# A hybrid decoder step: 120 unused words behind the constants, taken from the end of the big SBUF buffer

## The reference

```python
def expert(acc, ew):
    w1, b1, w2, b2, g_col = ew            # w1: 1024 x 2048, w2: 1024 x 1024, float32
    hh = xt @ w1 + b1
    glu = jnp.minimum(hh[:, 0::2], SWIGLU_LIMIT)
    lin = jnp.clip(hh[:, 1::2], -SWIGLU_LIMIT, SWIGLU_LIMIT)
    y = ((lin + 1.0) * (glu * jax.nn.sigmoid(SWIGLU_ALPHA * glu))) @ w2 + b2
    return acc + g_col[:, None].astype(y.dtype) * y, None
```

## Time and profile before

| | |
|---|---|
| median of three runs | 1518.68 us (1517.12, 1518.68 and 1520.63) |
| the profiled execution | 1514.24 us, of it 1512.4 us in the span of the profile |
| PE busy | 1357.4 us (90% of the span) |
| DVE busy | 472.7 us (31%) |
| ACT busy | 175.8 us (12%) |
| DMA over the span | 490.56 MB in 96,722 packets, 324 GB/s on the mean |

### The profile page before, as it was taken

One profiled execution on the slowest core, in us unless ns is written; L12 is line 12 of the kernel. 1 busy time (PEld: TensorE's weight loads), 2 busy tenths in 40 slices (PEclk: granted clock), 3 DMA queues, 4 the chain that ended last, 5 costly groups with the idle time before them and its releaser, 6 DMA issues.

```text
span 1512.4 us, 20016 instructions
## 1 busy us (share of the span) xinstructions
PE 1357.4 (90%) x8119; PEld 649.6 (43%) x8119; DVE 472.7 (31%) x1080; ACT 175.8 (12%) x343; POOL 49.5 (3%) x47
## 2 busy tenths in 40 slices
PE   8999769879997989999999988989989889899896
PEld 6667534334486444333333333333333333333332
DVE  1856556733124252122122113112221131122213
ACT  1143101221012430000000000000000000000002
POOL 0000210000000420000000000000000000000000
PEclk9999889889999999999999999999999999999999
DMA  9111545546366669999999999999999999999996
GB/s 360 38 62 48 196 153 196 203 140 251 145 244 220 237 264 416 397 413 415 417 418 414 420 415 415 420 415 417 418 414 419 416 415 420 415 417 418 415 419 238
DMA packets 96722, 490.56 MB, mean 324 GB/s; under 512 B 9307, under 2 KB 14527, under 8 KB 61754
## 3 DMA queue, kind: packets, MB, share of 16 engines
q1 hardware_dynamic: 94074, 468.80, 77.2%
q0 software_dynamic: 2304, 20.97, 3.6%
q10 hardware_dynamic: 296, 0.11, 0.0%
HBM read 483.91 MB, written 6.04 MB: 324 GB/s over the span
## 4 chain that ended last, share of the span: by engine, by line
PE 40%; DMA 18%; DVE 6%; SPq 3%; issue 2%; ACT 1%; POOL 1%; DVEq 0%
PE ps L2025 17%; DMA arena<-in_w_e 17%; PE ps L2062 13%; PE ps L2018 2%; SPq L1457 2%; PE ps L2050 1%; PE ps L2074 1%; DVE arena L2590 1%; DVE arena L2600 1%; DVE arena L2597 1%; DVE arena L2598 1%; DMA arena<-in_cache_mem_k 1%; PE ps L2090 1%; PE ps L2104 1%; SPq L1453 1%
## 5 line engine op out<-in xcount | busy, mean ns | idle before, releaser
L2025 PE MATMUL ps<-arena 128*64 128x512 f32 x2048 | 455.9, 595 | 29.1 <-DMA arena<-in_w_e 28.5
L2025 PEld LDWEIGHTS ps<-arena 128*64 128x64 f32 x2048 | 149.3, 137 | 311.7 <-issue 284.3
L2062 PE MATMUL ps<-arena 128*64 128x512 f32 x952 | 216.5, 609 | 1.2 <-ACT arena L2277 1.2
L2062 PEld LDWEIGHTS ps<-arena 128*64 128x64 f32 x952 | 78.0, 142 | 138.3 <-issue 125.4
L2597 DVE TENSOR_SCALAR arena<-ps 128x1024 f32<-128x1024 f32 x15 | 18.4, 1225 | 252.7 <-PE ps L2025 252.7
L2018 PE MATMUL ps<-arena 96*128 96x512 bf16 x96 | 39.6, 540 | 46.1 <-DVE arena L2590 46.1
L2609 DVE COPY arena<-ps 128x512 f32<-128x512 f32 x15 | 10.4, 692 | 218.8 <-PE ps L2062 218.8
L2615 DVE TENSOR_TENSOR res<-res,ps 128x512 f32<-128x512 f32 x60 | 41.3, 688 | 116.4 <-PE ps L2074 116.4
L1071 PE MATMUL ps<-arena 32*4 32x512 f32 x640 | 47.1, 641 | 14.9 <-PEq L1149 10.5
L2011 PE MATMUL ps<-arena 128*128 128x128 bf16 x768 | 54.2, 222 | 2.0 <-DVE arena L2564 2.0
L2011 PEld LDWEIGHTS ps<-arena 128*128 128x128 bf16 x768 | 49.7, 99 | 14.3 <-issue 12.2
(11 more groups left out here) (554 smaller groups left out, 1361.4 us busy)
## 6 DMA issues: line engine op xcount, KB each, us to landing
arena<-in_w_e SPq DMA_DIRECT2D x383, 1024.0 KB, 18.7
arena<-in_w_in SPq DMA_DIRECT2D x8, 1380.0 KB, 17.6
arena<-in_cache_mem_k SPq DMA_DIRECT2D x8, 1024.0 KB, 8.9
arena<-in_w_out SPq DMA_DIRECT2D x2, 2048.0 KB, 8.8
arena<-in_w_xk SPq DMA_DIRECT2D x1, 4096.0 KB, 16.0
arena<-in_w_xv SPq DMA_DIRECT2D x1, 4096.0 KB, 13.5
arena<-in_w_xq SPq DMA_DIRECT2D x1, 4096.0 KB, 23.3
arena<-in_cache_mem_v SPq DMA_DIRECT2D x1, 4096.0 KB, 16.5
```

What stands on the lines that cost most here:

```text
L2025: last = pe.matmul(ps[64 * x:64 * x + 64, c, :], xe[:, k, 64 * x:64 * x + 64], weights[x][:, c * 512:(c + 1) * 512], start=False, stop=(k ...
L2062: last = pe.matmul(ps[64 * x:64 * x + 64, 4 + c, :], aT[:, k, 64 * x:64 * x + 64], weights[x][:, j * D + c * 512:j * D + (c + 1) * 512], s ...
```

## The change

The table of constants gets 120 words more in each partition (480 bytes), which nothing reads, and `arena` gets 120 words less at its end. No instruction is added, taken away or moved, and no place inside `arena` changes, except one that is counted from its end (`AT_MORE = ARENA - ...`, a place for 1024 words of cached rotary keys), whose address stays as it was.

```diff
 C_HEAD = C_SUB + 1
-C_ALL = C_HEAD + H
-
-ARENA = 45680 + 3072 + 188
+C_ALL = C_HEAD + H + 120
+
+ARENA = 45680 + 3072 + 188 - 120
```

## The result

The changed kernel takes 1497.62 us (median of four runs, 1495.04 to 1505.40) against 1517.95 us (1517.12 to 1520.63): a ratio of 0.9872 with a 95% interval from 0.9833 to 0.9910. The forecast was 1518.7 us with a range down to 1513.5; the gain is 16 to 20 us. The profiled execution took 1497.29 us, of it 1495.5 us in the span, 16.9 us less than before.

The account below looks back on a forecast made before the run. The prediction took the expert stage to be bound by its weight queue at 417 GB/s. Its terms summed to 0 us on the profiled 1514.24 us; placed on the runs' median, the forecast was 1518.7 us, range 1513.5 to 1522.0.

Parts of the forecast that it names:

- the other parts: Longer constants load, moved stored states and PE, DVE and ACT operands moved by 480 bytes: each was to cost nothing.
- the cover of 86 us: Stored states land at 183.7 us, first read at 270.1 us; even a load 9.4 us longer was to cost nothing.
- From this I take the gain for a packet in the ring as nothing: Expert loop's weight landings: aligned ring places gain 0 us, bounded by 13.2 us of gain and 6.6 us of loss.
- block 7: The w_in block landing on a multiple of 512: 418.6 ns a packet, no cheaper than block 3's 416.9 ns.
- The sign of failure that I had named: Prediction fails if whole packets of 4096 and 8192 bytes profit from a clean start and a clean end together.
- The whole excess goes: Rival, expert loop: all 3.4 ns a packet come from landing, 13.2 us faster, 1505.5 us; chance 0.05 including a larger case.
- my line of prices: Packet price fitted from small and w_in packets: 8.2 ns fixed plus 0.03702 ns a byte, 236.5 ns for loop packets.
- One beat less: Rival, ring packets: an aligned start saves 32 bytes, 1.18 ns each, 4.6 us in all, 1514.1 us; chance 0.09.

Follow-up runs that it names:

- e9: Changed kernel plus six groups of 16 loads behind its last store; w_in blocks took 418.8, 415.8, 418.8 and 426.5 ns from 0, 128, 224 and 240.
- e7: Changed kernel plus ten groups of 20 loads behind its last store, varying start and length; 8192-byte packets took 309.0 ns from 0 and 314.6 from 32.
- e5: Kernel before with 24 unused words, so arena starts 128 past a multiple of 512; 1514.86 us against 1515.76, ratio 0.9991.
- e6: Kernel before with 56 unused words, so arena starts 256 past a multiple of 512; 1499.70 us against 1515.76, ratio 0.9879.
- e1: Kernel before with 8 unused words, so arena starts 64 past a multiple of 512; 1514.38 us against 1516.57, ratio 0.9991.

## Why the prediction was wrong

**What held.** The expert stage is bound by its queue, the engines stand at 1.02, and the landing of the fills is the only way for the change to act. The costs of the other parts held as well: constants and states stayed hidden. The constants landed at 6.7 + 30.5 = 37.2 us. The states did pay, 24 ns for a packet of four runs (a run of 512 bytes touches three lines from its new place and two from the old one, so 6 ns for each line more), and the cover of 86 us was real. The `w_in` blocks kept their 417 to 420 ns at their new places: 416.7, 418.2 and 420.1 in the stretches of the earlier trace rows. PE's and DVE's lines do not show in the difference: in the first stretch of 60 us PE is busy for 56.92 us in both kernels, and DVE for 12.92 to 12.93 us in all of them.

**The step that failed** is "From this I take the gain for a packet in the ring as nothing", and under it "I take nothing because block 7 is the nearest row". The blocks of `w_in` did start at eight different rests, and the three that I read cost the same within 2.5 ns, but they were no test. 11,040 is 43 x 256 + 32, so from every rest that is a multiple of 32 up to 224 a block touches 44 lines. 8192 is 32 x 256 and touches 32 lines from a multiple of 256 and 33 from anywhere else. The quantity that costs was constant in my test and changed in the ring. e9 shows this on the same data: from 240, where the block does touch a 45th line, it costs 7.7 ns more than from 224. I had noted that the blocks' ends are ragged wherever they start, and had left it as a remark; it should have made me count. The sign of failure that I had named, packets of 4096 and 8192 bytes that profit from a clean start and a clean end together, came true; clean ends matter only through the count.

**The rivals.** "The whole excess goes" was right in its effect: all that the loop's packets paid over my line of prices went away, and the time ended on its side. Its cause, ragged pieces at both ends, was wrong (8160 bytes from 16, ragged at both ends, cost nothing more; 8192 from 128, two halves of a line, cost 4), and its size was too small: 3.4 ns, where 5.0 were measured. My line ran through stores of 513 bytes and through the `w_in` packets at 416.9 ns, and the latter carry a surcharge of their own; through 8192 and 4096 bytes of e7 it is 309.0 - 159.2 = 149.8 ns for 4096 bytes, which gives 413.2 ns for 11,040. 256 packets a pair times 5.0 ns in 15.2 pairs are 19.5 us of packet time on each engine, beside 16 to 20 us in the kernel's time. "One beat less" named the right place with a price of 1.18 ns in place of 5.

The Trainium skill (DMA: Bandwidth & Descriptors, section How a descriptor splits into AXI transactions) has a descriptor cut into pieces of 256 bytes, each of which must start on a multiple of 256, so that an odd start can make one piece more. It speaks of what is read; here the landing address was varied. The count agrees with e7 in every row, and with the unit of e5 and e6. The price that the page names, the beats of the bytes below the start, does not: by it a start 128 past a line would cost four times one 32 past, where 4.2 and 5.6 ns were measured. I had used the page's price to judge the rule, and not its count.

**What stays open.** e1 and e5 lie 2.2 and 0.9 us below the kernel beside them, within their intervals; e7's 313.3 against 314.6 ns for 128 packets of 8192 bytes would make it 0.2 us a pair, which fits the 60.2 against 60.4 us of the queue, but the times do not show it. Why an additional line costs 3.4 ns in a short packet and up to 7.7 in a block of `w_in` was not settled. That the cost belongs to the landing address is shown, since in each comparison the sources began at the same places of their rows; by what mechanism it arises there is not. One row speaks against a cost of any odd SBUF address. The sample states are also stored from the place that went from a multiple of 256 to 224 past one, in 320.3 to 327.3 us of the changed kernel:

```profile
q1 hardware_dynamic: 3824, 1.95, 92.0%
```

That is 26.9 ns for a packet, where it was 27.2: as a source the odd place cost these short packets nothing.

## What to carry to other kernels

Where a stage goes at the pace of its loads, put the places that receive them on multiples of 256 bytes, and count the lines that each packet touches before and after: here a start 32 bytes off cost 1.2% of the kernel's time, and 480 unused bytes in each partition removed it. A test found inside a trace is one only if the quantity that is suspected varies in it; equal times at different offsets meant nothing, because the size made the count equal. When an excess over a simple fit stays unexplained in the stage that sets the end, its whole size belongs among the likely outcomes.

## What was not expected of the hardware

The cost of a landing packet goes in steps by lines of 256 bytes: 8192 bytes take 309.0 ns in 32 lines and 313.2 to 314.6 in 33, and 8160 bytes take 308 ns from 0, 16 and 32 alike, all within 32 lines. The size of the end pieces shows in the step: it is 4.2 to 4.4 ns for 8192 bytes where the smaller end piece has 128 or 64 bytes, and 5.6 to 6.9 ns for 8192 and 8160 bytes where it has 32 or 16. At equal counts a very small last piece seems to cost a little too: a block of `w_in` takes 415.8 ns from 128, where its end pieces have 128 and 160 bytes, and 418.8 from 0 or 224, where one has 32.
